# One matmul over both halves of the activations in a three-block transformer kernel

## The chip, the cores and the metric

The kernel runs on one core of one Trainium2 chip. The metric is the time of one execution on the device in microseconds. The change is compared with the kernel before by medians of several executions.

## What is computed

256 tokens of width 1024 in float32 go through a first block and then through a second one of two layers. The first block has a mixer (a gated delta rule and an S5 scan side by side), attention over a memory of 256 rows, and a gated feed-forward layer. Each layer of the second block has a self-attention (stick-breaking and block attention in the first, forgetting attention in the second), attention over a second memory with 4 heads of 64, and a feed-forward layer whose gate and value pass a causal convolution of three taps. All products with weights are in float32, and a root-mean-square norm stands ahead of each. Cut to the second block:

```python
def _rmsnorm(x, gain):
    x32 = x.astype(jnp.float32)
    y = x32 * lax.rsqrt(jnp.mean(x32 * x32, axis=-1, keepdims=True) + EPS)
    return (y * gain.astype(jnp.float32)).astype(x.dtype)
...
def memory_cross_attention(h, mem_h, w_q, w_kv, w_out):
...
    q = (h @ w_q).reshape(B, S, XA_HEADS, XA_HEAD_DIM)
    kv = (mem_h @ w_kv).reshape(B, M, 2, XA_HEADS, XA_HEAD_DIM)
    k, v = kv[:, :, 0], kv[:, :, 1]
    s = jnp.einsum('bshd,bmhd->bhsm', q, k).astype(jnp.float32) * (XA_HEAD_DIM ** -0.5)
    p = jax.nn.softmax(s, axis=-1).astype(h.dtype)
    o = jnp.einsum('bhsm,bmhd->bshd', p, v).reshape(B, S, XA_DIM)
    return o @ w_out
...
def second_block(x, mem, positions, norm_mix_g, norm_xa_g, norm_mem_g, norm_ffn_g,
...
    h = x
    for layer in range(DEPTH_2):
        n = layer // 2
        hn = rmsnorm(h, norm_mix_g[layer])
        if layer % 2 == 0:
            h = h + sb_moba_mixer(hn, positions, ab_w_in[n], ab_w_out[n])
        else:
            h = h + fox_mixer(hn, fox_w_in[n], fox_b_f[n], fox_w_out[n])
        h = h + memory_cross_attention(rmsnorm(h, norm_xa_g[layer]), rmsnorm(mem, norm_mem_g[layer]),
                                       xa_w_q[layer], xa_w_kv[layer], xa_w_out[layer])
        h = h + conv_ffn(rmsnorm(h, norm_ffn_g[layer]), ffn_w_up[layer], ffn_conv_w[layer],
                         ffn_conv_b[layer], ffn_w_down[layer])
    return rmsnorm(h, final_norm_g)
```

## The kernel before

**Tiling.** Activations lie feature by feature: h is 128 partitions x 8 chunks x 256 tokens. A product with a weight of 1024 x 1024 is 8 outputs (m) of 8 blocks (k) of 128 x 128 each. Weights come in slots of 8 blocks (128 x 1024, 512 KB): SyncE loads a slot into w_raw (6 buffers), ScalarE copies it rounded to float32r into w_hi (L1127), and VectorE (L1686) or, for every third slot, GpSimd (L2500) subtracts that from the raw one into w_lo. Both have 3 buffers, and ScalarE waits for the slot three back to be used up before it makes the next w_hi. Activations are split the same way, a_hi by ScalarE (L1153) and a_lo by VectorE (L1698), for attention's outputs b_hi and b_lo.

**Three matmuls per block.** The helper three (L418) multiplies one block of weights: w_hi with x_hi, w_hi with x_lo, w_lo with x_hi, each 256 columns wide and all added up in the same 256 columns of a bank. A bank holds 512 columns of float32. Where the tokens are the stationary side (the value products, tok_slot), the moving side is 512 columns of weights. The first stages (w_in, and the keys and values of the second memory, up to x_v) take raw weights in one matmul.

**Stages in order of time.** w_in with the delta rule and the scan (to 141 us), x_v and x_k (keys and values of the first memory, to about 235), glu, w_out, x_q with attention, x_o, ffn0 (342 to 528), ab_v, ab_q and ab_k with attention, ab_o, m_q0, memory attention, m_o0, ffn1 (693 to 885), fox_v, fox_f, fox_q and fox_k, fox_o, m_q1, memory attention, m_o1, ffn2, the last norm.

**Output projections.** residual, written once for each engine, computes w_out, x_o, ab_o, fox_o (K = 8) and m_o0, m_o1 (K = 2). TensorE's fm makes one output m after the other in two banks in turn. VectorE adds it to h (L2115) and frees the bank, then makes a_lo of the chunk before (L1698) and adds its squares up (L2105; not for m_o0 and m_o1). ScalarE makes a_hi (L1153) and the square (L1143) as soon as h is there. Ahead of each h both engines call ahead, which makes w_hi (ScalarE) or w_lo (VectorE, if the slot is not GpSimd's) up to three slots beyond the one in use. The order within each engine is that of the program text, and every wait is on a semaphore.

**Scaled products.** x_k, x_q, ab_q, ab_k, fox_q, fox_k, m_q0 and m_q1 are read from their bank once and multiplied by the norm's rstd (scaled, L1858). In the feed-forward layers (ffn) the gate and the value of each of 22 steps are two outputs of 8 blocks, read and scaled at L2245; the down product of a step is 8 blocks that add up in banks 4 to 7 over all steps. In ffn0 a SiLU and a product follow; in ffn1 and ffn2 the convolution comes between.

## Time and profile before

| | us |
|---|---|
| median of 3 executions | 1260.03 |
| lowest and highest | 1256.9 and 1260.96 |
| the profiled execution, as timed | 1257.22 |
| its span in the trace | 1255.3 |
| TensorE busy | 1194.8 (95%) |
| VectorE busy | 808.1 (64%) |
| ScalarE busy | 656.8 (52%) |
| GpSimd busy | 265.0 (21%) |

PE is TensorE, DVE VectorE, ACT ScalarE, POOL GpSimd. Matmuls are pipelined: the duration of one overlaps with the next, so its price in a row is the distance from start to start. A time in brackets behind an instruction is how long its engine sat idle before it, and what ended that. L numbers are lines of the kernel before.

### The profile page before, as it was taken

To read this page: it belongs to the slowest core of one execution; us is meant where nothing else is said; L and a number is where in the kernel's file an instruction comes from. 1 tells how busy PE (TensorE), PEld (TensorE's weight loads), DVE (VectorE), ACT (ScalarE), POOL (GpSimd) and SP (SyncE) were. 2 spreads that over 40 slices of the span, in tenths; PEclk is the share of its full clock that TensorE was granted. 3 is DMA by queue.
4 is the path that set the end of the run, shared out by engine and by line. 5 is a ranking of instruction groups with operands and counts; after the bars stand their busy time and mean duration, and the time that the engine had idled before them with its cause. 6 is when DMAs were issued, how large, how long until landed. Compare 5 with 4: busy or idle time off the path is not lost.

```text
span 1255.3 us, 24604 instructions
## 1 busy us (share of the span) xinstructions
PE 1194.8 (95%) x10064; PEld 1119.2 (89%) x10064; DVE 808.1 (64%) x1426; ACT 656.8 (52%) x1128; POOL 265.0 (21%) x172
## 2 busy tenths in 40 slices
PE   7999999899999999999998899999999988999997
PEld 6888778799899999998886899999889877999997
DVE  4886655564655454567866677677665576776776
ACT  3443633653644444465455655555655566555554
POOL 4030000121222322321120222322221211232231
PEclk9999899999999999999999999999999999999999
DMA  8443322353565565643343466565443342656651
GB/s 320 128 134 119 108 96 86 101 169 101 155 199 175 181 189 181 184 135 102 117 135 102 119 200 176 181 192 178 150 141 116 115 151 84 187 182 187 181 176 48
DMA packets 51518, 187.58 MB, mean 149 GB/s; under 512 B 5712, under 2 KB 5840, under 8 KB 51024
## 3 DMA queue, kind: packets, MB, share of 16 engines
q1 hardware_dynamic: 51408, 186.02, 47.8%
q8 instruction: 80, 1.31, 0.4%
q14 instruction: 30, 0.25, 0.1%
HBM read 184.95 MB, written 1.05 MB: 148 GB/s over the span
## 4 chain that ended last, share of the span: by engine, by line
PE 83%; DVE 7%; ACT 4%; issue 3%; POOL 1%; DMA 0%; DVEq 0%; SPq 0%; ACTq 0%
PE banks L418 62%; PE banks L448 7%; ACT w_hi L1127 2%; PE banks L491 2%; DVE w_lo L1686 1%; PE banks L476 1%; PE banks L924 1%; PE banks L938 1%; POOL w_lo L2500 1%; DVE h L2115 1%; PE banks L539 1%; PE banks L904 1%; DVE gates L2105 1%; PE banks L841 1%; DVE a_lo L1698 1%
## 5 line engine op out<-in xcount | busy, mean ns | idle before, releaser
L418 PE MATMUL banks<-a_hi,w_hi 128*128 128x256 f32 x1432 | 412.2, 288 | 10.1 <-ACT arena L1426 4.2
L2500 POOL TENSOR_TENSOR w_lo<-w_raw,w_hi 128x1024 fp32r<-128x1024 f32 x99 | 240.6, 2430 | 836.0 <-ACT w_hi L1127 836.0
L1127 ACT ACTIVATE w_hi<-w_raw 128x1024 fp32r<-128x1024 f32 x313 | 328.4, 1050 | 157.4 <-PE banks L418 157.3
L418 PE MATMUL banks<-a_lo,w_hi 128*128 128x256 f32 x1432 | 405.9, 283 | 0.0
L418 PE MATMUL banks<-a_hi,w_lo 128*128 128x256 f32 x1432 | 405.8, 283 | 0.0
L1686 DVE TENSOR_TENSOR w_lo<-w_raw,w_hi 128x1024 fp32r<-128x1024 f32 x214 | 264.5, 1236 | 66.7 <-ACT w_hi L1127 66.5
L418 PEld LDWEIGHTS banks<-a_hi,w_hi 128*128 128x128 f32 x1432 | 275.4, 192 | 14.9 <-ACT arena L1426 4.6
L418 PEld LDWEIGHTS banks<-a_lo,w_hi 128*128 128x128 f32 x1432 | 275.5, 192 | 0.4
L418 PEld LDWEIGHTS banks<-a_hi,w_lo 128*128 128x128 f32 x1432 | 275.3, 192 | 0.0
L418 PE MATMUL banks<-b_hi,w_hi 128*128 128x256 f32 x880 | 254.9, 290 | 16.2 <-DVE h L2115 3.9
L418 PE MATMUL banks<-b_hi,w_lo 128*128 128x256 f32 x880 | 249.9, 284 | 0.0
L418 PE MATMUL banks<-b_lo,w_hi 128*128 128x256 f32 x880 | 249.9, 284 | 0.0
L418 PEld LDWEIGHTS banks<-b_hi,w_hi 128*128 128x128 f32 x880 | 169.5, 193 | 22.4 <-issue 12.2
L418 PEld LDWEIGHTS banks<-b_lo,w_hi 128*128 128x128 f32 x880 | 169.7, 193 | 0.3
L418 PEld LDWEIGHTS banks<-b_hi,w_lo 128*128 128x128 f32 x880 | 169.6, 193 | 0.0
L1569 ACT ACTIVATE arena<-arena,pars 128x256 f32<-128x256 f32 x88 | 53.0, 602 | 132.9 <-DVE arena L2245 132.9
L2245 DVE TENSOR_TENSOR arena<-banks,rstd 128x256 f32<-128x256 f32 x132 | 55.8, 423 | 103.2 <-PE banks L418 93.4
L448 PE MATMUL banks<-early,w_raw 128*128 128x256 f32 x400 | 92.2, 390 | 7.6 <-DMA w_raw<-in_weights 7.6
L2250 DVE SCALAR_TENSOR_TENSOR arena<-arena,pars 128x255 f32<-128x255 f32 x88 | 59.1, 672 | 60.7 <-ACT arena L1569 60.7
L448 PEld LDWEIGHTS banks<-early,w_raw 128*128 128x128 f32 x400 | 77.0, 195 | 19.4 <-DMA w_raw<-in_weights 7.6
L1153 ACT ACTIVATE a_hi<-h,pars 128x256 fp32r<-128x256 f32 x64 | 32.5, 507 | 63.4 <-DVE h L2115 53.3
L1584 ACT ACTIVATE b_hi<-arena 128x256 fp32r<-128x256 f32 x66 | 27.6, 418 | 36.6 <-DVE arena L2264 36.6
(379 smaller groups left out, 1326.7 us busy)
## 6 DMA issues: line engine op xcount, KB each, us to landing
w_raw<-in_weights SPq DMA_DIRECT2D x342, 512.0 KB, 3.6
h<-in_x SPq DMA_DIRECT2D x1, 1024.0 KB, 5.1
arena<-in_mem SPq DMA_DIRECT2D x1, 1024.0 KB, 12.3
early<-in_mem SPq DMA_DIRECT2D x1, 1024.0 KB, 14.3
out_h<-h SPq DMA_DIRECT2D x4, 256.0 KB, 2.7
...
```

The source lines that it names most:

```text
L418: ins = mm(out, l, r, start=start and n == 0, stop=stop and n == 2, skip_group_check=check)
L448: ins = mm(out, raw(s, b % 8), x[:, k, :], start=n == 0, stop=n == K - 1)
L476: ins = mm(out, x[:, k, cols], raw(s, b * w % 8, w), start=k == 0, stop=k == K - 1)
L491: ins = mm(bank[2][:, 0:T] if out is None else out, ONES_D[:] if by is None else by, squares, start=m == 0, stop=m == KD - 1)
L1127: do(WHI[:, n % SPLIT_SLOTS, :], RAW[:, n % RAW_SLOTS, :], ACT.Copy).then_inc(*inc("w_hi_made", ("w_hi", n)))
L1153: do(x[0][:, m, :], src, ACT.Copy, scale=par(g, m)).then_inc(*inc("input_hi", ("a_hi", tag, m)))
L1569: do(FC[:, 2 * (f % 2) + g, :], FS[:, 2 * (f % 3) + g, :], ACT.Identity, scale=par(f"cw{conv}", 88 + g * NF + f), bias=par(f"cb{conv}", g ...
L1584: do(BH[:, f % 3, :], FA[:, f % 2, :], ACT.Copy).then_inc(*inc("ffn_act_hi", ("act_hi", tag, f)))
L1686: v.tensor_tensor(WLO[:, n % SPLIT_SLOTS, :], RAW[:, n % RAW_SLOTS, :], WHI[:, n % SPLIT_SLOTS, :].bitcast(F32), ALU.subtract).then_inc(*i ...
L2245: v.tensor_tensor(x, acc(t)[:, 0:T], R[:], ALU.mult).then_inc(*inc("ffn_scaled", ("fs", tag, f, g), ("acc", t)))
L2250: step(v.scalar_tensor_tensor(c[:, 1:T], x[:, 0:T - 1], par(f"cw{conv}", 44 + g * NF + f), c[:, 1:T], ALU.mult, ALU.add), label="ffn_conv")
L2500: g.tensor_tensor(WLO[:, n % SPLIT_SLOTS, :], RAW[:, n % RAW_SLOTS, :], WHI[:, n % SPLIT_SLOTS, :].bitcast(F32), ALU.subtract).then_inc(*i ...
```

## The change

The halves of the activations come to lie in one tensor each (a_parts, b_parts, halves outermost). A new helper, joint, takes the place of three in most products with weights as the stationary side: one matmul of w_hi with both halves, 512 columns, into the whole bank, and one of w_lo with x_hi, 256 columns, into its first half. The bank then holds two partial results per output, and its reader adds them: for h two additions with a wait between them (the second frees the bank); in scaled and in ffn0's gate and value a reduction over pairs into the destination, then the multiplication by rstd there. Left as they were: glu, fox_f, the gates and values of ffn1 and ffn2 (ONE_HALF), every down product, and all products with tokens as the stationary side. In this version the matmuls fall from 8766 to 7710 instructions in the program, by 1056. Not shown below are the sites where only x[0] and x[1] became x[:, 0] and x[:, 1] on ScalarE.

```diff
--- before.py
+++ after.py
@@ -235,8 +235,8 @@
                 "p (a b) -> p a b", a=KD) for i in range(3))
         WHI = sb("w_hi", [P, SPLIT_SLOTS, 1024], F32R)
         WLO = sb("w_lo", [P, SPLIT_SLOTS, 1024], F32R)
-        AH, AL = sb("a_hi", [P, KD, T], F32R), sb("a_lo", [P, KD, T], F32R)
-        BH, BL = sb("b_hi", [P, KD, T], F32R), sb("b_lo", [P, KD, T], F32R)
+        A, B = (sb(n, [P, 2, KD, T], F32R) for n in ("a_parts", "b_parts"))
+        (AH, AL), (BH, BL) = ((x[:, 0, :, :], x[:, 1, :, :]) for x in (A, B))
         RAW = sb("w_raw", [P, RAW_SLOTS, 1024])
         H = sb("h", [P, KD, T])
         K1, V1 = sb("k1", [P, KD, T]), sb("v1", [P, TT, D])
@@ -292,8 +292,9 @@
 
             return bank[(6, 6, 6, 6, 6, 2, 3, 4)[p]]
 
-        A = (AH, AL)
-        B = (BH, BL)
+        def halves(key):
+
+            return acc(key).rearrange("p (a b) -> p a b", a=2)
 
 
         QKV = area(0, 12, T)
@@ -418,12 +419,19 @@
                     ins = mm(out, l, r, start=start and n == 0, stop=stop and n == 2, skip_group_check=check)
                 return ins
 
+            def joint(out, w, x, k, start, stop):
+
+
+                mm(out.rearrange("p (a b) -> p a b", a=2), w[0], x[:, :, k, :], start=start, stop=stop,
+                   skip_group_check=True)
+                return mm(out[:, 0:T], w[1], x[:, 0, k, :], start=False, stop=stop, skip_group_check=True)
+
             def blocks(s, b, n=1):
                 c = slice(b * P, (b + n) * P)
                 return WHI[:, s % SPLIT_SLOTS, c], WLO[:, s % SPLIT_SLOTS, c]
 
             def pair(x, k, cols=slice(0, T)):
-                return x[0][:, k, cols], x[1][:, k, cols]
+                return x[:, 0, k, cols], x[:, 1, k, cols]
 
             def raw(s, b, n=1):
                 return RAW[:, s % RAW_SLOTS, b * P:(b + n) * P]
@@ -432,7 +440,7 @@
 
 
                 K = SHAPE[name][0]
-                out = acc_take((name, m))[:, 0:T]
+                out = acc_take((name, m))
                 for n, k in enumerate(range(K)):
                     b = m * K + k
                     s = SLOT[name, b // 8]
@@ -445,9 +453,11 @@
                             sums(k)
                         pe.wait_ge(*at(x_ready(k)))
                     if whole(s):
-                        ins = mm(out, raw(s, b % 8), x[:, k, :], start=n == 0, stop=n == K - 1)
+                        ins = mm(out[:, 0:T], raw(s, b % 8), x[:, k, :], start=n == 0, stop=n == K - 1)
+                    elif name in ONE_HALF:
+                        ins = three(out[:, 0:T], blocks(s, b % 8), pair(x, k), n == 0, n == K - 1)
                     else:
-                        ins = three(out, blocks(s, b % 8), pair(x, k), n == 0, n == K - 1)
+                        ins = joint(out, blocks(s, b % 8), x, k, n == 0, n == K - 1)
                     ev = ([("slot", s)] if (m * K + n) % 8 == 7 else []) + ([(name, m)] if n == K - 1 else [])
                     if ev:
                         ins.then_inc(*inc("product_done", *ev))
@@ -862,12 +872,15 @@
                 for f in range(NF + 1):
                     if f < NF:
                         for g in range(2):
-                            out = acc_take((name, 2 * f + g))[:, 0:T]
+                            out = acc_take((name, 2 * f + g))
                             slot_ready(s)
                             for k in range(KD):
                                 if f == 0 and g == 0:
                                     pe.wait_ge(*at(("a_lo", tag, k)))
-                                ins = three(out, blocks(s, k), pair(A, k), k == 0, k == KD - 1)
+                                if name in ONE_HALF:
+                                    ins = three(out[:, 0:T], blocks(s, k), pair(A, k), k == 0, k == KD - 1)
+                                else:
+                                    ins = joint(out, blocks(s, k), A, k, k == 0, k == KD - 1)
                             ins.then_inc(*inc("product_done", ("slot", s), (name, f, g)))
                             s += 1
                             if f == 0 and g == 0:
@@ -1695,12 +1708,12 @@
 
             def lo_gained(tag, m, x, src, g):
                 dve.wait_ge(*at(("a_hi", tag, m)))
-                v.scalar_tensor_tensor(x[1][:, m, :], src, par(g, m), x[0][:, m, :].bitcast(F32),
+                v.scalar_tensor_tensor(x[:, 1, m, :], src, par(g, m), x[:, 0, m, :].bitcast(F32),
                                        ALU.mult, ALU.subtract).then_inc(*inc("input_lo", ("a_lo", tag, m)))
 
             def lo(tag, m, x, src, key=("a_hi", "a_lo")):
                 dve.wait_ge(*at((key[0], tag, m)))
-                v.tensor_tensor(x[1][:, m, :], src, x[0][:, m, :].bitcast(F32), ALU.subtract).then_inc(
+                v.tensor_tensor(x[:, 1, m, :], src, x[:, 0, m, :].bitcast(F32), ALU.subtract).then_inc(
                     *inc("input_lo", (key[1], tag, m)))
 
             v.memset(ONES_D[:], 1.0 / D).then_inc(*inc("vector_step", "ones"))
@@ -1855,8 +1868,14 @@
             def scaled(name, m, dst, r, scale=1.0):
                 t = (name, m)
                 dve.wait_ge(*at((name, m)))
-                v.scalar_tensor_tensor(dst, acc(t)[:, 0:T], scale, r, ALU.mult, ALU.mult).then_inc(
-                    *inc("scaled_out", (name, "scaled", m), ("acc", t)))
+                if whole(SLOT[name, 0]):
+                    v.scalar_tensor_tensor(dst, acc(t)[:, 0:T], scale, r, ALU.mult, ALU.mult).then_inc(
+                        *inc("scaled_out", (name, "scaled", m), ("acc", t)))
+                    return
+                step(v.tensor_reduce(dst, halves(t).rearrange("p a b -> p b a"), AX.X, ALU.add), ("acc", t),
+                     label="halves_summed")
+                v.scalar_tensor_tensor(dst, dst, scale, r, ALU.mult, ALU.mult).then_inc(
+                    *inc("scaled_out", (name, "scaled", m)))
 
 
             turn = delta_banks(bank)
@@ -2112,7 +2131,8 @@
                     ahead(FIRST[name] + (m * K + K - 1) // 8)
                     t = (name, m)
                     dve.wait_ge(*at((name, m)))
-                    step(v.tensor_tensor(H[:, m, :], H[:, m, :], acc(t)[:, 0:T], ALU.add),
+                    step(v.tensor_tensor(H[:, m, :], H[:, m, :], halves(t)[:, 0, :], ALU.add), label="halves_summed")
+                    step(v.tensor_tensor(H[:, m, :], H[:, m, :], halves(t)[:, 1, :], ALU.add),
                          ("h", tag, m), ("acc", t), label="h_made")
                     if m:
                         lo_gained(tag, m - 1, A, H[:, m - 1, :], g)
@@ -2242,8 +2262,13 @@
                                 dve.wait_ge(*at(("fa", tag, f - 3)))
                             x = FS[:, 2 * (f % 3) + g, :]
                             t = (name, 2 * f + g)
-                            v.tensor_tensor(x, acc(t)[:, 0:T], R[:], ALU.mult).then_inc(
-                                *inc("ffn_scaled", ("fs", tag, f, g), ("acc", t)))
+                            if conv is not None:
+                                v.tensor_tensor(x, acc(t)[:, 0:T], R[:], ALU.mult).then_inc(
+                                    *inc("ffn_scaled", ("fs", tag, f, g), ("acc", t)))
+                            else:
+                                step(v.tensor_reduce(x, halves(t).rearrange("p a b -> p b a"), AX.X, ALU.add), ("acc", t),
+                                     label="halves_summed")
+                                v.tensor_tensor(x, x, R[:], ALU.mult).then_inc(*inc("ffn_scaled", ("fs", tag, f, g)))
                             if conv is not None:
                                 c = FC[:, 2 * (f % 2) + g, :]
                                 dve.wait_ge(*at(("fc", tag, f, g)))
@@ -2579,6 +2604,8 @@
 
 SUMMED = ("xa", "f0", "xa0", "xa1")
 
+ONE_HALF = ("glu", "fox_f", "ffn1", "ffn2")
+
 POOL_SUMMED = ("mem1", "mem2")
 
 sq_before = {}
```

The order of TensorE's instructions in x_o, from its last block into ffn0's first output, before (waits in brackets):

```order
L418 MATMUL banks<-b_hi,w_hi 128x256
L418 MATMUL banks<-b_lo,w_hi 128x256
L418 MATMUL banks<-b_hi,w_lo 128x256
L418 MATMUL banks<-a_hi,w_hi 128x256 [waits w_lo_made,input_lo,w_hi_made,h_made]
L418 MATMUL banks<-a_lo,w_hi 128x256
L418 MATMUL banks<-a_hi,w_lo 128x256
L418 MATMUL banks<-a_hi,w_hi 128x256 [waits input_lo]
```

and after:

```order
L425 MATMUL banks<-b_parts,w_hi 128x512
L427 MATMUL banks<-b_parts,w_lo 128x256
L425 MATMUL banks<-a_parts,w_hi 128x512 [waits w_lo_made,input_lo,w_hi_made,h_made]
L427 MATMUL banks<-a_parts,w_lo 128x256
L425 MATMUL banks<-a_parts,w_hi 128x512 [waits input_lo]
```

Three matmuls became two; the waits stand on the first of each block as before.

VectorE at the end of an output projection and the start of the next stage (x_o, then ffn0), before; squares are added at L2105, w_lo made at L1686:

```order
L1686 TENSOR_TENSOR w_lo<-w_raw,w_hi 128x1024 [waits w_hi_made]
L2115 TENSOR_TENSOR h<-h,banks 128x256 [waits product_done]
L1698 SCALAR_TENSOR_TENSOR a_lo<-h,pars,a_hi 128x256 [waits input_hi,h_made]
L2105 TENSOR_TENSOR gates<-gates,squares 128x256 [waits squares_summed,squares]
L1698 SCALAR_TENSOR_TENSOR a_lo<-h,pars,a_hi 128x256 [waits input_hi]
L2105 TENSOR_TENSOR gates<-gates,squares 128x256 [waits squares_summed,squares]
L2245 TENSOR_TENSOR arena<-banks,rstd 128x256 [waits product_done,rstd]
```

and after:

```order
L1699 TENSOR_TENSOR w_lo<-w_raw,w_hi 128x1024 [waits w_hi_made]
L2134 TENSOR_TENSOR h<-h,banks 128x256 [waits product_done]
L2135 TENSOR_TENSOR h<-h,banks 128x256 [waits halves_summed]
L1711 SCALAR_TENSOR_TENSOR a_parts<-h,pars,a_parts 128x256 [waits input_hi,h_made]
L2124 TENSOR_TENSOR gates<-gates,squares 128x256 [waits squares_summed,squares]
L1711 SCALAR_TENSOR_TENSOR a_parts<-h,pars,a_parts 128x256 [waits input_hi]
L2124 TENSOR_TENSOR gates<-gates,squares 128x256 [waits squares_summed,squares]
L2269 TENSOR_REDUCE arena<-banks 128x256 [waits product_done,rstd]
L2271 TENSOR_TENSOR arena<-arena,rstd 128x256 [waits halves_summed]
```

Between w_lo and a_lo now stand two additions, the second waiting for the first; the event h_made is the second's.

VectorE in m_q0, ahead of the memory attention, before:

```order
L1858 SCALAR_TENSOR_TENSOR arena<-banks,rstd 128x256 [waits product_done,rstd]
L1686 TENSOR_TENSOR w_lo<-w_raw,w_hi 128x1024 [waits w_hi_made]
L1858 SCALAR_TENSOR_TENSOR arena<-banks,rstd 128x256 [waits product_done]
L2138 TENSOR_REDUCE small<-banks 128x2 [waits scores_done] x3
L2146 RECIPROCAL small<-small 128x2 [waits exp_done]
```

and after:

```order
L1875 TENSOR_REDUCE arena<-banks 128x256 [waits product_done,rstd]
L1877 SCALAR_TENSOR_TENSOR arena<-arena,rstd 128x256 [waits halves_summed]
L1699 TENSOR_TENSOR w_lo<-w_raw,w_hi 128x1024 [waits w_hi_made]
L1875 TENSOR_REDUCE arena<-banks 128x256 [waits product_done]
L1877 SCALAR_TENSOR_TENSOR arena<-arena,rstd 128x256 [waits halves_summed]
```

Each scaling is two instructions now; the first reduction waits for the rstd, which only the second instruction needs.

## Rows read from the trace of the kernel before

**Rows 1.** the page: busy time of each engine and TensorE's largest group of matmuls
```profile
PE 1194.8 (95%) x10064; PEld 1119.2 (89%) x10064; DVE 808.1 (64%) x1426; ACT 656.8 (52%) x1128; POOL 265.0 (21%) x172
L418 PE MATMUL banks<-a_hi,w_hi 128*128 128x256 f32 x1432 | 412.2, 288 | 10.1 <-ACT arena L1426 4.2
```

**Rows 2.** stretches; us, busy time (count) per engine, granted clock, DMA share, GB/s
```profile
342.00:517.00 175.00, 174.89 (x1456) 174.57 (x1456) 87.59 (x131) 82.02 (x110) 49.89 (x21) 1.00 0.60 185
549.00:635.00 86.00, 83.86 (x628) 74.53 (x628) 67.54 (x102) 47.36 (x83) 16.82 (x7) 1.00 0.40 117
712.00:882.00 170.00, 170.00 (x1417) 170.00 (x1418) 123.28 (x199) 93.74 (x137) 46.36 (x20) 1.00 0.62 184
920.00:997.00 77.00, 76.39 (x624) 67.71 (x622) 39.02 (x73) 40.82 (x99) 14.82 (x6) 1.00 0.40 124
```

**Rows 3.** order of time, PE, value products within fox: start us, us, engine, line
```profile
984.02 0.39 PE L418 MATMUL banks<-w_hi,a_hi 128*128 128x512 f32 x1
987.88 0.39 PE L418 MATMUL banks<-w_lo,a_hi 128*128 128x512 f32 x1
```

**Rows 4.** order of time, one turn of the loop in x_o, VectorE and ScalarE
```profile
335.72 0.41 DVE L2115 TENSOR_TENSOR h<-h,banks 128x256 f32<-128x256 f32 x1
...
336.17 0.51 ACT L1153 ACTIVATE a_hi<-h,pars 128x256 fp32r<-128x256 f32 x1 [1.62 <-DVE h L2115]
...
336.89 1.04 ACT L1127 ACTIVATE w_hi<-w_raw 128x1024 fp32r<-128x1024 f32 x1
...
337.96 1.23 DVE L1686 TENSOR_TENSOR w_lo<-w_raw,w_hi 128x1024 fp32r<-128x1024 f32 x1 [0.98 <-ACT w_hi L1127]
339.11 0.41 DVE L2115 TENSOR_TENSOR h<-h,banks 128x256 f32<-128x256 f32 x1
```

**Rows 5.** additions into h in w_out, x_o, ab_o, fox_o: busy, mean ns | idle before
```profile
L2115 DVE TENSOR_TENSOR h<-h,banks 128x256 f32<-128x256 f32 x8 | 3.3, 414 | 0.8 <-PE banks L418 0.8
L2115 DVE TENSOR_TENSOR h<-h,banks 128x256 f32<-128x256 f32 x8 | 3.3, 414 | 2.7 <-PE banks L418 2.7
L2115 DVE TENSOR_TENSOR h<-h,banks 128x256 f32<-128x256 f32 x8 | 3.3, 414 | 1.0 <-PE banks L418 1.0
L2115 DVE TENSOR_TENSOR h<-h,banks 128x256 f32<-128x256 f32 x8 | 3.3, 414 | 2.4 <-PE banks L418 2.4
```

**Rows 6.** order of time, VectorE: second h of x_o and of fox_o
```profile
319.21 0.42 DVE L2115 TENSOR_TENSOR h<-h,banks 128x256 f32<-128x256 f32 x1 [2.21 <-PE banks L418]
...
1000.46 0.42 DVE L2115 TENSOR_TENSOR h<-h,banks 128x256 f32<-128x256 f32 x1 [1.66 <-PE banks L418]
```

**Rows 7.** order of time, VectorE in m_o0: two additions in a row
```profile
684.06 0.87 DVE L2115 TENSOR_TENSOR h<-h,banks 128x256 f32<-128x256 f32 x2
```

**Rows 8.** VectorE's reductions over 512 columns of a bank
```profile
L2138 DVE TENSOR_REDUCE small<-banks 128x2 f32<-128x512 f32 x12 | 8.0, 686 | 4.9 <-PE banks L818 4.5 <-PE banks L1033 0.5
```

**Rows 9.** order of time, VectorE in m_q0
```profile
668.72 0.42 DVE L1858 SCALAR_TENSOR_TENSOR arena<-banks,rstd 128x256 f32<-128x256 f32 x1 [2.48 <-ACT rstd L1160]
```

**Rows 10.** order of time, m_o0 and the start of ffn1
```profile
686.83 0.42 DVE L2115 TENSOR_TENSOR h<-h,banks 128x256 f32<-128x256 f32 x1 [0.35 <-PE banks L418]
...
693.44 1.02 DVE L1698 SCALAR_TENSOR_TENSOR a_lo<-h,pars,a_hi 128x256 fp32r<-128x256 f32 x2
...
696.09 0.59 PE L491 MATMUL banks<-squares,ones_d 128*128 128x256 f32 x2
```

**Rows 11.** order of time in x_o: VectorE beside GpSimd
```profile
328.30 2.69 POOL L2500 TENSOR_TENSOR w_lo<-w_raw,w_hi 128x1024 fp32r<-128x1024 f32 x1 [7.01 <-ACT w_hi L1127]
...
328.64 2.64 DVE L2105 TENSOR_TENSOR gates<-gates,squares 128x256 f32<-128x256 f32 x1
```

**Rows 12.** PE after a wait before w_out, and the stretch behind it
```profile
241.46 0.38 PE L418 MATMUL banks<-a_hi,w_hi 128*128 128x256 f32 x1 [4.23 <-ACT arena L1426]
...
241.60:245.10 3.50, 3.50 (x18) 3.50 (x19) 1.09 (x3) 1.59 (x3) 2.31 (x1) 0.53 0.00 0
```

**Rows 13.** order of time, PE: ffn0's first output waits for a_lo
```profile
340.10 0.38 PE L418 MATMUL banks<-a_hi,w_hi 128*128 128x256 f32 x1 [0.81 <-DVE a_lo L1698]
```

4 lines of the change are left out of this document (2 added, 2 removed).

## The prediction

> **What bounds the kernel now.** Read the busy line first: TensorE works in 95% of the span, VectorE in 64% [rows 1]. So nearly everything that shortens TensorE's stream counts, and everything that adds to VectorE is free as long as TensorE does not have to wait. Which of the two holds differs from stage to stage, so the second view is the table of stretches [rows 2]. In ffn0 (342 to 517 us) TensorE is busy 174.89 of 175.00 us with 1456 matmuls, 120.1 ns each, and VectorE only 87.59. ffn1's inner stretch is as dense with VectorE at 123.28 of 170: a VectorE filled to 73% does not hold TensorE there. Attention's ab stretch has VectorE at 67.54 of 86, fox at 39.02 of 77.
>
> The third view, the order of time, shows stages that TensorE does not bound. In the four output projections with K = 8 (w_out, x_o, ab_o, fox_o) the additions into h are 3.39 us apart (335.72 to 339.11) without VectorE waiting for TensorE [rows 4]: h, then ScalarE's a_hi at 336.17, square, w_hi at 336.89, then VectorE's w_lo at 337.96, then the next h. It is a closed loop, since w_hi stands behind the square on ScalarE, and h behind w_lo on VectorE. One block of 24 matmuls needs 24 x 0.120 = 2.88 us, so TensorE is the faster one in such a turn. Where the slot's w_lo is GpSimd's (one in three), the turn is short and VectorE waits for the product: in all 0.8, 2.7, 1.0 and 2.4 us in the four stages [rows 5]. At the end of x_o TensorE already waits 0.81 us for a_lo [rows 13].
>
> **The joint matmul.** A dense matmul of 256 columns takes 120 ns from start to start [rows 2]. For 512 columns, 17 starts from 984.02 to 987.88 are 227 ns apart [rows 3]. Two of 256 columns are 240, so a block of one 512 and one 256 takes 347 instead of 360 ns: 13 ns less. The bounds are 0 (the small one takes 133 ns behind a large one) and 26 (what a small one takes beyond half of a large one and its 13 is hidden too). The change converts 1056 blocks: 352 in ffn0, 64 each in x_k, w_out, x_q, x_o, ab_q, ab_k, ab_o, fox_q, fox_k, fox_o, and 16 each in m_q0, m_o0, m_q1, m_o1. That is 13.7 us of TensorE's time, of which only the blocks in dense stages count.
>
> The rows give a fixed part of some 13 ns per matmul. The Trainium skill, page "TensorE: Matmul & The Clock Gate", section "Back-to-back issue gap", gives N/2.4 + 2.5 ns for matmuls in a row, under which a block would save 2.5 ns, 2.6 us over all 1056; the trace's 120 ns for 256 columns is above its 109, and the trace decides.
>
> **Where the gain stays.** ffn0: 352 x 13 ns = 4.6 us. VectorE gets 44 reductions of 512 columns, at 0.69 us by the nearest row [rows 8], in place of the read of 256, and a multiplication of 0.42 behind it: 44 x 0.73 = 32 us on top of 87.59, 120 of 175, what ffn1 bears without a gap. x_q: 0.8. x_k: 0.8, of which 0.2 stay, since its reductions lie between steps of the delta chain. ab_q and ab_k: 1.7; VectorE grows by 16 x 0.73 = 12 to 79 of 86 [rows 2], so I take 1.1 for stalls, the price of a whole new scaling step once on the path (0 to 5), leaving 0.6. fox_q and fox_k: 1.7 less 0.7 for one reduction ahead of the first scores, 1.0; there VectorE has room (39 of 77). Sum: 4.6 + 0.8 + 0.2 + 0.6 + 1.0 = **7.2 us gained**.
>
> **Output projections.** The second addition and its wait on the first lie in the loop, since a_hi and the square wait for the second. Its price is the pitch of two additions in a row, 0.87 - 0.42 = 0.45 us [rows 7]. Eight are 3.6. VectorE's waits for the product pay part back. In x_o the 2.21 in front of the second h, in fox_o the 1.66 [rows 6], swallow only what the first h lost (0.45); other waits count in full. w_out 3.6 - 0.8 = 2.8; x_o 3.6 - 0.45 - 0.5 = 2.65; ab_o 3.6 - 1.0 = 2.6; fox_o 3.6 - 0.45 - 0.7 = 2.45; together **10.5 us lost**. What TensorE saves in these stages is worth nothing: the last a_lo is late anyway [rows 13]. Queued behind the second addition are a_lo, the sum of squares and the next w_lo; who waits is TensorE's first output of the next stage. Bounds: 4 x 0.45 = 1.8, if only the last h counts, and 4 x 3.6 = 14.4.
>
> **m_o0 and m_o1** (K = 2, six matmuls per output). The same 0.45 per h makes the fourth h end 4 x 0.45 - 0.35 = 1.45 late and the last 3.0. The last a_lo ends at 693.44 + 1.02 = 694.46, and ffn1's first block passes to the sums at 696.09, so 1.4 of it is slack [rows 10]: 1.6 each, **3.2 us lost** (0 to 6).
>
> **m_q0 and m_q1.** The scaling stands between the rstd and the attention scores [rows 9]: 0.69 + 0.05 + 0.42 instead of 0.42, twice, less 0.2 to 0.5 in which w_lo waits for w_hi anyway: 1.0 each, **2.0 us lost** (0 to 3).
>
> **Clock.** TensorE's idle time at the end of an output projection grows from 0.8 to about 3 us. Before w_out it stood for 4.23 us, and then ran at 0.53 of full speed, the level of 1.2 GHz, for 3.5 us [rows 12]; 18 matmuls there cost 3.50 instead of 2.16, so 1.3 us. I take one such fall in the six stage ends: **1.3 us lost** (0 to 8).
>
> **The sum.** -7.2 + 10.5 + 3.2 + 2.0 + 1.3 = +9.8. The profiled execution took 1257.22 us (a span of 1255.3 and 1.9 around it), so 1267.0 beside it. It lies 2.8 below the median of 1260.03 and near the lowest of three (1256.9); the forecast is a little over the sum, **1268 us**.
>
> **Rivals.**
> - *The collisions with GpSimd go, and it gets faster.* In the output projections VectorE operations with two operands in SBUF stand still while GpSimd makes a w_lo: 2.64 us for 0.42 of work [rows 11], and the four stages hold nine such stretches, of 0.9 to 2.3 us and 15 in all. The new additions read a bank and do not stand still (the 32 additions of those stages all take 0.41 [rows 5]). If the later h moves a_lo and the sum out from beside GpSimd in nearly all cases, 14 us come back: 1254. From six avoided stretches on (6 x 1.7 = 10) the loss of 9.8 is gone. Against it: w_hi, which starts GpSimd, hangs on the same h and moves with it. 0.11.
> - *It nearly cancels.* The loop's loss is half, because the second addition fills time in which VectorE stands beside GpSimd: 10.5 becomes 5, no fall of the clock, 4 us less in the two small stages: 1260. 0.13.
> - *A block saves nothing*, the fixed part staying with the load of weights. Then 736 blocks x 13 ns = 9.6 us of the gain fall away: 1278. TensorE's part would show 360 ns per block. Against it: the 227 ns for 512 columns include a load each. By the page's 2.5 ns per block it would be 1275. 0.10.
> - *The reduction is dear.* With two elements per output instead of 256 it may cost 1.4 instead of 0.69: VectorE in ab 67.54 + 16 x 1.4 = 90 > 86, some 10 us there and 3 in m_q: 1281. 0.05.
>
> **How the numbers follow.** The forecast has 0.61 and spans 1263 to 1274. Of it 0.60 is above 1263.8; a measurement of this kernel can tell some 0.3%, 3.8 us, from no change. Slower: 0.60 + 0.15 from the last two rivals = 0.75. Same: the second rival, 0.13, and 0.01: 0.14. Faster: 0.11. The range of 1256 to 1278 leaves out the first rival (0.11) and the dear reduction with the upper part of the third (0.08).
>
> **What would show it.** In the changed profile: ffn0's stretch dense and shorter by about 4.6 us; the additions into h in x_o 3.8 us apart in w_lo turns, and the stage about 2.6 longer; reductions of 0.69; TensorE waiting 2 us and more for a_lo at each stage end; the start of ffn1 later by 1.6 within its stage. Wrong would be: gaps in ffn0 behind a bank, the h pitch still 3.4, or ab's stretch longer than 86.

## Result and the profile after

The changed kernel is slower: a median of 1274.67 us in four runs (1274.03 to 1279.11) against 1259.82 for the kernel before, and a ratio of 1.0134 with a 95% interval of 1.011 to 1.0158. The forecast was 1268 us. The direction and the place of the largest loss were right; the size was not: 14.9 us were lost by the medians, 16.9 by the ratio, where 8 to 10 were forecast. The profiled execution has a span of 1273.4 us against 1255.3, 18.1 more.

The page of the changed kernel, its busy line and the groups that take the place of the three matmuls (compare [rows 1]):

```profile
PE 1193.5 (94%) x9008; PEld 1062.4 (83%) x9008; DVE 899.5 (71%) x1570; ACT 660.2 (52%) x1128; POOL 265.9 (21%) x172
...
L425 PE MATMUL banks<-a_parts,w_hi 128*128 128x512 f32 x704 | 257.7, 407 | 7.6 <-DVE a_parts L1711 6.9
...
L425 PE MATMUL banks<-b_parts,w_hi 128*128 128x512 f32 x352 | 132.0, 414 | 18.7 <-POOL w_lo L2525 9.0
```

TensorE has 1056 instructions less and is busy 1.3 us less. VectorE has gained 91 us. The waits in front of the wide matmuls are now for VectorE and GpSimd: 18.7 us where attention's outputs are multiplied.

VectorE's additions into h mark the ends of the stages, since they come in the same order in both kernels. First the kernel before (start, duration, engine, line; the last addition of w_out, the first behind ffn0, the last of ab_o, the first behind ffn1, the last of fox_o, the first behind ffn2), then the changed one, with x_o's last, which is in [rows 4] for before, as second row:

```profile
272.22 0.41 DVE L2115 TENSOR_TENSOR h<-h,banks 128x256 f32<-128x256 f32 x1
...
527.72 0.42 DVE L2278 TENSOR_TENSOR h<-h,banks 128x256 f32<-128x256 f32 x1 [1.14 <-PE banks L418]
...
664.24 0.41 DVE L2115 TENSOR_TENSOR h<-h,banks 128x256 f32<-128x256 f32 x1
...
887.63 0.42 DVE L2278 TENSOR_TENSOR h<-h,banks 128x256 f32<-128x256 f32 x1 [1.14 <-PE banks L418]
...
1018.97 0.42 DVE L2115 TENSOR_TENSOR h<-h,banks 128x256 f32<-128x256 f32 x1 [0.51 <-PE banks L418]
...
1242.74 0.42 DVE L2278 TENSOR_TENSOR h<-h,banks 128x256 f32<-128x256 f32 x1 [1.14 <-PE banks L418]
```

```profile
276.16 0.42 DVE L2135 TENSOR_TENSOR h<-h,banks 128x256 f32<-128x256 f32 x1
...
345.01 0.42 DVE L2135 TENSOR_TENSOR h<-h,banks 128x256 f32<-128x256 f32 x1
...
532.67 0.42 DVE L2303 TENSOR_TENSOR h<-h,banks 128x256 f32<-128x256 f32 x1 [1.14 <-PE banks L419]
...
673.51 0.42 DVE L2135 TENSOR_TENSOR h<-h,banks 128x256 f32<-128x256 f32 x1
...
899.75 0.42 DVE L2303 TENSOR_TENSOR h<-h,banks 128x256 f32<-128x256 f32 x1 [1.13 <-PE banks L419]
...
1033.92 0.42 DVE L2135 TENSOR_TENSOR h<-h,banks 128x256 f32<-128x256 f32 x1
...
1261.03 0.42 DVE L2303 TENSOR_TENSOR h<-h,banks 128x256 f32<-128x256 f32 x1 [1.13 <-PE banks L419]
```

The differences of these starts give the ledger, with the prediction's terms beside it:

| stretch | before | after | difference | forecast |
|---|---|---|---|---|
| start to w_out's last h | 272.22 | 276.16 | +3.94 | -0.2 + 2.8 = +2.6 |
| x_q, x_o | 66.89 | 68.85 | +1.96 | -0.8 + 2.65 = +1.85 |
| ffn0 | 188.61 | 187.66 | -0.95 | -4.6 |
| ab, ab_o | 136.52 | 140.84 | +4.32 | -0.6 + 2.6 = +2.0 |
| m_q0, m_o0, ffn1 | 223.39 | 226.24 | +2.85 | 1.0 + 1.6 = +2.6 |
| fox, fox_o | 131.34 | 134.17 | +2.83 | -1.0 + 2.45 = +1.45 |
| m_q1, m_o1, ffn2 | 223.77 | 227.11 | +3.34 | 1.0 + 1.6 = +2.6 |
| the end | 12.56 | 12.37 | -0.19 | 0 |
| falls of the clock, no place given | | | | +1.3 |
| sum | | | +18.10 | +9.8 |

Three stretches hold most of the miss: ffn0 (3.65 us), ab (2.3) and fox (1.4). The stretch up to w_out misses 1.3 more; this lies in glu, where TensorE's granted clock stood at 0.50 for seven microseconds (241 to 248) where it had been three and a half before [rows 12], behind the same wait of 4.23 us. It is scatter and not the change: the profiled executions of experiments 2, 3, 5 and 7 show the long fall too, those of 1, 4, 6, 8 and 9 the short one, and glu is the same in all.

**The loop of h is as foretold.** VectorE in x_o after the change, to be compared with [rows 4]:

```profile
340.71 0.42 DVE L2134 TENSOR_TENSOR h<-h,banks 128x256 f32<-128x256 f32 x1
341.16 0.42 DVE L2135 TENSOR_TENSOR h<-h,banks 128x256 f32<-128x256 f32 x1
...
343.42 1.23 DVE L1699 TENSOR_TENSOR w_lo<-w_raw,w_hi 128x1024 fp32r<-128x1024 f32 x1 [0.94 <-ACT w_hi L1140]
344.56 0.41 DVE L2134 TENSOR_TENSOR h<-h,banks 128x256 f32<-128x256 f32 x1
```

One turn takes 3.85 us (340.71 to 344.56) where it took 3.39.

**A joint block saves 7 ns, not 13.** TensorE in ffn0, one joint block and the start of the next:

```profile
403.17 0.40 PE L425 MATMUL banks<-a_parts,w_hi 128*128 128x512 f32 x1
403.40 0.28 PE L427 MATMUL banks<-a_parts,w_lo 128*128 128x256 f32 x1
403.52 0.40 PE L425 MATMUL banks<-a_parts,w_hi 128*128 128x512 f32 x1
```

The wide one holds TensorE for 236 ns and the narrow one for 117 (means over 269 and 252 pairs between 356 and 500 us), together 353; three narrow ones took 360.

**The multiplication of a scaling has changed its operands.** Before, it read a bank and the rstd. Now the reduction reads the bank, and the multiplication reads two operands in SBUF. The view of one line's instructions gives their shortest, median and longest duration in ns, before and after:

```profile
L1858 DVE SCALAR_TENSOR_TENSOR arena<-banks,rstd x44: 406/424/425, 276.7 to 1027.0; 128x256 f32<-128x256 f32 x44
```

```profile
L1877 DVE SCALAR_TENSOR_TENSOR arena<-arena,rstd x44: 424/425/2604, 281.4 to 1042.8; 128x256 f32<-128x256 f32 x44
...
L1875 DVE TENSOR_REDUCE arena<-banks x44: 673/691/693, 280.6 to 1042.1; 128x256 f32<-128x512 f32 x44
```

No multiplication of before took over 425 ns. After the change seven take 1.13 to 2.60 us, 10.4 us more than their work, and each of them stands beside a w_lo of GpSimd. The dearest, with GpSimd's row, and TensorE's wait behind it (L990 rotates the queries and keys; it waits for the bank of the rotation before, which VectorE reads right behind this multiplication, L2343):

```profile
611.94 2.38 POOL L2525 TENSOR_TENSOR w_lo<-w_raw,w_hi 128x1024 fp32r<-128x1024 f32 x1 [9.83 <-ACT w_hi L1140]
...
611.29 0.68 DVE L1875 TENSOR_REDUCE arena<-banks 128x256 f32<-128x512 f32 x1
612.00 2.60 DVE L1877 SCALAR_TENSOR_TENSOR arena<-arena,rstd 128x256 f32<-128x256 f32 x1
...
615.09 0.67 PE L990 MATMUL banks<-arena 128*128 128x256 f32 x2 [1.59 <-DVE arena L2343]
...
616.00:620.00 4.00, 4.00 (x21) 3.31 (x22) 3.90 (x9) 0.81 (x1) 0.00 (x0) 0.58 0.22 87
```

The last row is the stretch behind the gap (us, then busy time and count per engine, granted clock, DMA share, GB/s): the granted clock is 0.58, that is the level of 1.2 GHz for most of it. The Trainium skill has the rule: by "SBUF — State Buffer", section "Who interferes with whom", a VectorE instruction with two SBUF inputs contends with a GpSimd instruction that reads SBUF, and a tensor_reduce never does. The trace agrees on both: of the 96 reductions of two halves some 30 run beside a w_lo, and none takes over 694 ns.

But most of this standing beside GpSimd is not new. In ab the kernel before has seven stretched instructions of VectorE, 9.4 us beyond their work, on a_lo, the rotation, the stick-breaking scores and a norm; after the change there are eight, of 12.1 us, and five of them are the new multiplication. The kernel before, at the same place in ab as the row of 2.60 us above, in the rotation:

```profile
607.97 2.52 DVE L2320 TENSOR_TENSOR arena<-arena 128x256 f32<-128x256 f32 x1
```

In fox they grow from one stretch of 1.8 us to five of 9.0, two of them on the new multiplication and two on one that was there before and has been moved beside a w_lo, the scaling of the attention weights (before, then after):

```profile
L2181 DVE TENSOR_TENSOR arena<-arena,small 128x256 f32<-128x256 f32 (+1 forms) x16 | 8.2, 554 | 0.3
...
L2201 DVE TENSOR_TENSOR arena<-arena,small 128x256 f32<-128x256 f32 (+1 forms) x16 | 12.5, 825 | 0.3
```

### The profile page after: what moved, and what is told of

It reads as the page before. It is cut to its first block, busy times and chain, and to the rows that moved or that the text cites. A ratio compares the mean times of both kernels' runs of the same rounds, so it can differ in the third digit from the quotient of the medians.

```text
span 1273.4 us, 22636 instructions
## 1 busy us (share of the span) xinstructions
PE 1193.5 (94%) x9008; PEld 1062.4 (83%) x9008; DVE 899.5 (71%) x1570; ACT 660.2 (52%) x1128; POOL 265.9 (21%) x172
## 4 chain that ended last, share of the span: by engine, by line
PE 75%; DVE 14%; ACT 6%; issue 3%; DMA 0%; POOL 0%; DVEq 0%; SPq 0%; ACTq 0%
PE banks L419 38%; PE banks L425 12%; PE banks L456 7%; PE banks L427 6%; DVE w_lo L1699 4%; ACT w_hi L1140 2%; PE banks L501 2%; DVE h L2135 1%; DVE gates L2124 1%; PE banks L486 1%; DVE h L2134 1%; DVE arena L1875 1%; DVE a_parts L1711 1%; PE banks L951 1%; PE banks L937 1%
## 5 line engine op out<-in xcount | busy, mean ns | idle before, releaser
L419 PE MATMUL banks<-a_parts,w_hi 128*128 128x256 f32 x1456 | 268.0, 286 | 8.3 <-ACT arena L1439 4.2
L425 PE MATMUL banks<-a_parts,w_hi 128*128 128x512 f32 x704 | 257.7, 407 | 7.6 <-DVE a_parts L1711 6.9
L419 PEld LDWEIGHTS banks<-a_parts,w_hi 128*128 128x128 f32 x1456 | 229.6, 194 | 10.3 <-ACT arena L1439 4.6
L419 PE MATMUL banks<-a_parts,w_lo 128*128 128x256 f32 x728 | 207.0, 284 | 0.0
L419 PE MATMUL banks<-b_parts,w_hi 128*128 128x256 f32 x1056 | 193.2, 283 | 6.8 <-DVE w_lo L1699 3.5
L427 PE MATMUL banks<-a_parts,w_lo 128*128 128x256 f32 x704 | 198.2, 282 | 0.0
L419 PEld LDWEIGHTS banks<-b_parts,w_hi 128*128 128x128 f32 x1056 | 164.3, 191 | 8.7 <-issue 5.8
L425 PEld LDWEIGHTS banks<-a_parts,w_hi 128*128 128x128 f32 x704 | 133.3, 189 | 42.0 <-DVE a_parts L1711 9.5
L425 PE MATMUL banks<-b_parts,w_hi 128*128 128x512 f32 x352 | 132.0, 414 | 18.7 <-POOL w_lo L2525 9.0
L419 PE MATMUL banks<-b_parts,w_lo 128*128 128x256 f32 x528 | 149.4, 283 | 0.0
L419 PEld LDWEIGHTS banks<-a_parts,w_lo 128*128 128x128 f32 x728 | 140.8, 193 | 0.0
L427 PEld LDWEIGHTS banks<-a_parts,w_lo 128*128 128x128 f32 x704 | 134.0, 190 | 0.3
L419 PEld LDWEIGHTS banks<-b_parts,w_lo 128*128 128x128 f32 x528 | 101.0, 191 | 0.0
L425 PEld LDWEIGHTS banks<-b_parts,w_hi 128*128 128x128 f32 x352 | 66.9, 190 | 40.6 <-issue 12.9
L427 PE MATMUL banks<-b_parts,w_lo 128*128 128x256 f32 x352 | 99.3, 282 | 0.0
```

Source lines behind the costliest of these rows:

```text
L419: ins = mm(out, l, r, start=start and n == 0, stop=stop and n == 2, skip_group_check=check)
L425: mm(out.rearrange("p (a b) -> p a b", a=2), w[0], x[:, :, k, :], start=start, stop=stop, skip_group_check=True)
L427: return mm(out[:, 0:T], w[1], x[:, 0, k, :], start=False, stop=stop, skip_group_check=True)
```

## The experiments

Except where before.py is named, they start from a version of the changed kernel in which each product chooses between three matmuls with one addition or scaling, as before, and the joint product with two, by the list ONE_HALF. The stage lengths beside each come from the same additions into h.

**1. ffn0 alone.**

```diff
-ONE_HALF = ("glu", "fox_f", "ffn1", "ffn2")
+ONE_HALF = ("glu", "fox_f", "ffn1", "ffn2", "w_out", "x_o", "ab_o", "fox_o", "m_o0", "m_o1",
+            "x_k", "x_q", "ab_q", "ab_k", "fox_q", "fox_k", "m_q0", "m_q1")
```

> The joint product in the gate and value of ffn0 alone (352 of the 1056 blocks); everything else reads and multiplies as in the kernel before. Theory of the prediction (13 ns per block, VectorE's 44 reductions and multiplications hidden): 4.6 us faster than the kernel before. Theory from the trace of the changed kernel (a joint block has a pitch of 353 ns against 360, so 7 ns): 2.5 us faster. Rival (VectorE's extra 32 us are not hidden, since two of its multiplications stood beside GpSimd): 0 to 2 us slower.

Measured: 1255.85 us against 1256.82, a ratio of 0.9998 (0.9984 to 1.0013). The time can't tell a gain of 0 from one of 2 us, the trace can: ffn0 (337.44 to 524.94) takes 187.50 us where it took 188.61, 1.1 less. TensorE's gaps in it, none of which the kernel before has:

```profile
346.17 0.51 PE L425 MATMUL banks<-a_parts,w_hi 128*128 128x512 f32 x1 [0.32 <-DVE arena L2270]
...
349.86 0.36 PE L419 MATMUL banks<-b_parts,w_hi 128*128 128x256 f32 x1 [0.61 <-ACT w_hi L1140]
...
523.95 0.36 PE L419 MATMUL banks<-b_parts,w_hi 128*128 128x256 f32 x1 [0.45 <-DVE b_parts L2299]
```

352 blocks x 7 ns are 2.5 us; less 0.32 + 0.61 + 0.45 leaves 1.1. In the 170 us between, VectorE's extra 32 us cost nothing. At both ends they do cost: the first two outputs wait for the rstd and are then read one after the other, and at the end nothing lies between the last scaling and the last down product.

**2. The six output projections alone** (the list holds all but these).

> The joint product and the two additions in the six output projections alone (w_out, x_o, ab_o, fox_o, m_o0, m_o1). By the prediction's terms: 10.5 + 3.2 + 1.3 = 15.0 us slower than the kernel before. Theory from the trace of the changed kernel: 2.2, 2.45, 2.3 and 2.4 in the four long ones, 3.2 in each short one, and 1.6 us for a fall of the clock behind x_o: 17 us slower. Rival (most of the loss sits in the scaled products and ffn0): under 8 us.

Measured: 1272.62 us, 15.8 over the kernel before, ratio 1.0122 (1.0098 to 1.0146). By stage, first to last h: w_out +2.63, x_o +2.56, ab_o +2.35, fox_o +2.27, m_o0 +3.20, m_o1 +3.46. ffn1 behind m_o0 is as long as before within 0.1 us (194.54, 194.64). This is nearly the whole loss of the change, and the prediction's three terms for it, 15.0 us, were nearly right in sum.

**3. The scaled products alone.**

> The joint product in the scaled products alone (x_k, x_q, ab_q, ab_k, fox_q, fox_k, m_q0, m_q1). By the prediction's terms: 0.8 + 0.2 + 0.6 + 1.0 gained against 2.0 lost, 0.6 us faster. Theory from the trace of the changed kernel (the new multiplication has two operands in SBUF and stands still beside GpSimd, seven times, 10.4 us in all; one of them opens a gap of 1.6 us on TensorE with a fall of the clock behind it): 2 to 5 us slower, with the loss in the ab stretch.

Measured: 1260.04 us, 3.2 over the kernel before, ratio 1.0019 (1.0003 to 1.0034). x_q is 0.64 us shorter. ab, from the first h behind ffn0 to ab_o's first (525.99 to 641.32), is 1.37 us longer than before, fox 0.51. Eight multiplications stood beside GpSimd, 12.7 us beyond their work. The prediction's terms fall here: they gave a gain of 0.6 us. The clock did not fall in ab, though the same gap of 1.58 us stood there as in the changed kernel.

**4. Two steps without the joint product.**

```diff
 # before.py, residual on VectorE
-step(v.tensor_tensor(H[:, m, :], H[:, m, :], acc(t)[:, 0:T], ALU.add),
+step(v.scalar_tensor_tensor(H[:, m, :], acc(t)[:, 0:T], 0.5, H[:, m, :], ALU.mult, ALU.add))
+step(v.scalar_tensor_tensor(H[:, m, :], acc(t)[:, 0:T], 0.5, H[:, m, :], ALU.mult, ALU.add),
      ("h", tag, m), ("acc", t), label="h_made")
```

> The kernel before with its three matmuls per block, in which h takes each product in two instructions of half the product, the second waiting for the first; the same in the second block's six output projections as in the first. It tells the second addition apart from the joint product. If the second step in the loop is the whole loss of the output projections: as slow as the kernel with the joint product in the output projections alone, within 2 us, some 15 to 18 us over the kernel before. If the joint product carries a part (its larger matmuls hold a bank for longer): clearly less than that kernel, by 4 us and more.

Measured: 1275.31 us, 18.5 over the kernel before, ratio 1.0147 (1.0118 to 1.0177), whose interval overlaps that of the second experiment; the medians are 2.7 us apart, a little more than the 2 expected, the profiled spans 0.1 (1272.1 and 1272.2). VectorE in w_out, the joint product (experiment 2) and then this kernel:

```profile
264.71 0.41 DVE L2135 TENSOR_TENSOR h<-h,banks 128x256 f32<-128x256 f32 x1
265.15 0.42 DVE L2136 TENSOR_TENSOR h<-h,banks 128x256 f32<-128x256 f32 x1
...
267.65 2.60 DVE L2124 TENSOR_TENSOR gates<-gates,squares 128x256 f32<-128x256 f32 x1
```

```profile
264.77 0.42 DVE L2115 SCALAR_TENSOR_TENSOR h<-banks,h 128x256 f32<-128x256 f32 x1
265.22 0.42 DVE L2116 SCALAR_TENSOR_TENSOR h<-banks,h 128x256 f32<-128x256 f32 x1
...
267.73 2.60 DVE L2105 TENSOR_TENSOR gates<-gates,squares 128x256 f32<-128x256 f32 x1
```

The two run alike to 0.1 us over the whole projection, so in the four long projections the second step is the whole loss, and what TensorE saves there is worth nothing. The rows also settle the rival on GpSimd: the sum of squares still stands beside a w_lo for 2.60 us. In a_lo and the sums together such stretches cost 17.3 us before, 19.5 in experiment 2 and 19.1 after the change; in the four long projections, which the rival was about, there are nine again, of 15.9 us in place of 15.0.

**5. ffn0 with the wide ones first.**

```diff
-                                    ins = joint(out, blocks(s, k), A, k, k == 0, k == KD - 1)
+                                    mm(out.rearrange("p (a b) -> p a b", a=2), blocks(s, k)[0], A[:, :, k, :],
+                                       start=k == 0, stop=k == KD - 1, skip_group_check=True)
+                            if name not in ONE_HALF:
+                                for k in range(KD):
+                                    ins = mm(out[:, 0:T], blocks(s, k)[1], A[:, 0, k, :], start=False,
+                                             stop=k == KD - 1, skip_group_check=True)
```

> As the kernel with the joint product in ffn0 alone, but within an output TensorE first runs the eight matmuls of 512 columns (w_hi with both halves), then the eight of 256 (w_lo with x_hi). It asks where the 6 ns per block went that the prediction counted and the trace doesn't show (353 ns per block instead of 347). If the dear thing is the change between the two widths (a wide one behind a narrow one takes 236 ns, not 227): eight blocks take 8 x 347 ns, ffn0 4.6 us shorter than before and 2.1 shorter than with the alternating order. If a wide matmul with the two halves side by side (2 x 256 columns from two places) is itself dearer than one with 512 columns in a row: 236 ns within the wide ones too, and ffn0 as in the alternating order, 2.5 us shorter than before.

Measured: 1256.00 us against 1256.98, ratio 0.9991 (0.9977 to 1.0005). TensorE in ffn0, one output:

```profile
405.04 2.00 PE L883 MATMUL banks<-a_parts,w_hi 128*128 128x512 f32 x8
406.88 1.12 PE L887 MATMUL banks<-a_parts,w_lo 128*128 128x256 f32 x8
407.83 0.40 PE L883 MATMUL banks<-a_parts,w_hi 128*128 128x512 f32 x1
```

Eight wide ones take 1.84 us, 230 ns each, and eight narrow ones 0.95, 119 each: 349 ns per block against 353 in turns and 360 with three. So both readings were half right. A wide one with its halves in two places costs 3 ns more than one with 512 columns in a row [rows 3], where however the moving side is the weights and not the activations, so that the two places are not shown to be the reason. In turns with narrow ones a wide one takes 6 more and the narrow one 2 less.

This run's ffn0 took 187.59 us, no less than in experiment 1, because the clock fell in it: about 0.5 for three of the microseconds from 340 to 343. Experiment 7 has the same ffn0, behind the same wait of 1.58 us, without a fall: 186.42. The fall cost 1.2 us, and the order of the two widths brings 1.1.

**6. ab without GpSimd.** A pair of kernels: before, and experiment 3, each with

```diff
 def lo_on_pool(s):
     if s < FIRST["glu"]:
         return False
+    if FIRST["ab_q"] <= s < FIRST["ab_o"]:
+        return False
```

> The kernel before, in which VectorE and not GpSimd makes all w_lo of the ab stretch (ab_v, ab_q, ab_k): the reference for the next kernel. VectorE gets some eight w_lo of 1.22 us, and loses its stretches beside GpSimd. Every theory: within 4 us of the kernel before; its own time decides nothing, the difference to the next kernel does.

> The joint product in the scaled products alone, with all w_lo of the ab stretch made by VectorE. Theory: ab loses time because the new multiplication has both operands in SBUF and stands still beside GpSimd. Then without GpSimd no multiplication takes over 0.6 us in ab, and ab (from the end of ffn0 to the first h of ab_o) is no longer than in the reference of the same kind, within 0.7 us, where it was 1.5 us longer with GpSimd. Rival (VectorE is simply too full by the reductions): the stretch is longer than in its reference by 2 us and more, since VectorE now has 8 us more to do.

Seven of the nine w_lo that GpSimd made in this stretch go to VectorE; the two at its ends stay. Measured: 1254.89 us (ratio to the kernel before 0.9992, 0.9977 to 1.0007) and 1256.05 us (0.9999, 0.9987 to 1.0011). The multiplications of the ab stretch (545 to 637 us) in the kernel of experiment 3 and in its sister without GpSimd (busy, mean ns | idle before; in the sister all lines stand two lower, so that its L1879 is the multiplication and its L1877 the reduction):

```profile
L1877 DVE SCALAR_TENSOR_TENSOR arena<-arena,rstd 128x256 f32<-128x256 f32 x16 | 14.3, 896 | 0.6
```

```profile
L1879 DVE SCALAR_TENSOR_TENSOR arena<-arena,rstd 128x256 f32<-128x256 f32 x16 | 6.8, 426 | 0.6
...
619.44 0.47 PE L421 MATMUL banks<-w_hi,a_parts 128*128 128x512 f32 x1 [0.95 <-DVE arena L1877]
```

Their mean falls from 896 to 426 ns, so GpSimd's w_lo was what held them. ab is 112.21 us long against 111.31 in the reference of its kind (528.12 to 640.33, 524.02 to 635.33): 0.90 longer, where it was 1.37 with GpSimd. That is just outside the 0.7 of the theory and well under the 2 of its rival. The collisions are a third of ab's loss in this pair. For the rest a queue is the likely cause: the middle of ab was full before. The stretch of 602 to 624 us, where VectorE's busy time is the third, in the kernel before and in the sister without GpSimd:

```profile
602.00:624.00 22.00, 21.72 (x165) 18.70 (x161) 20.16 (x35) 9.72 (x24) 4.78 (x2) 1.00 0.39 119
```

```profile
602.00:624.00 22.00, 20.80 (x120) 16.53 (x119) 20.52 (x41) 11.32 (x32) 0.00 (x0) 1.00 0.29 99
```

20.16 of 22 us, 92%, where the whole stretch showed 79% [rows 2]. There a reduction more has little room, and TensorE waits 0.95 us for the reduction's bank. In the reference without GpSimd VectorE is busy for 19.48 of the same 22 us, and TensorE has no gap there. That the fullness costs the remaining 0.90 us is argued from these rows; no run takes it away.

**7. ffn0 (wide first) and x_q alone.**

> A version that should beat both: the joint product in ffn0 (wide ones first, then narrow ones) and in x_q alone. From the traces so far x_q is 0.6 us shorter with it and ffn0 2.5 to 4.6: 3 to 5 us faster than the kernel before (ratio 0.996 to 0.998). Rival (VectorE's extra work, or the clock behind the start of ffn0, takes it back): no difference.

Measured: 1255.55 us against 1256.98, ratio 0.9989 (0.9974 to 1.0005). The stages are shorter as expected, ffn0 by 2.19 us and x_q by 0.63, but the clock scatters the whole by more.

**8. The same, and ab without GpSimd.**

> The joint product in ffn0 (wide ones first) and x_q alone, and VectorE makes all w_lo of the ab stretch, so that no work of the ab stretch stands beside GpSimd. The traces give: ffn0 1.0 to 1.5 us shorter, x_q 0.6, ab 2.6: 4 to 5 us faster than the kernel before (ratio 0.996 to 0.997). Rival (the times of one program scatter by several us with the clock in the first 250 us, and the gain of each part was never outside the noise of the medians): a ratio of 0.998 to 1.000.

Measured: 1252.24 us (1249.87 to 1257.31) against 1257.25, ratio 0.9964 (0.9951 to 0.9978). This version beats both kernels. ab takes 110.90 us where it took 113.96. The largest part of the gain has nothing to do with the joint product: it is VectorE freed from GpSimd. Experiment 6 has it alone, ab 2.65 us shorter, though its time could not show it: there the stretches beside GpSimd in ab fall from 9.4 us to 1.3.

**9. All but the output projections.**

> The changed kernel with the six output projections (w_out, x_o, ab_o, fox_o, m_o0, m_o1) back at three matmuls and one addition: the joint product in ffn0 and in the scaled products together. If the parts add up: the 0 to 1 us that ffn0 alone gained and the 2.4 to 3.2 us that the scaled products alone lost, so 1.5 to 3 us slower than the kernel before (ratio 1.001 to 1.0025). The prediction's terms: 5.2 us faster (0.996). If the loss of the whole change (17 us) is more than its parts, because the later ends of the output projections disturb ffn0 and ab: no slower than the kernel before.

Measured: 1259.99 us, 2.7 over the kernel before, ratio 1.0026 (1.0015 to 1.0036), where the prediction's terms gave 5.2 gained. fox is 1.84 us longer here and not 0.5: the clock fell in it at 913 us, behind a wait of 2.12. The parts add up: 0.26% here and 1.22% in the projections are 1.48%, the whole change 1.34% (1.1 to 1.58).

## The prediction, point by point

**Where the miss is.** By the medians of the parts, the output projections lost 15.8 us where 15.0 were forecast (experiment 2), the scaled products lost 3.2 where 0.6 were to be gained (experiment 3), and ffn0 gained 1.0 where 4.6 were forecast (experiment 1). So the forecast failed in the gain: some 3.6 us in ffn0 and 3.8 in the scaled products.

**What bounds the kernel: right, with one hole.** Dense stages bear VectorE's work, projections do not. The hole is the average: ab was judged by 67.54 of 86 us, and in its middle VectorE was busy for 20.16 of 22 (experiment 6).

**The joint matmul: the term of 13 ns was too large.** It was put together from the pitch of narrow ones among narrow ones and of wide ones in a row. In the mixture a block saves 7 ns (353 against 360), 7.4 us over 1056 blocks instead of 13.7. The bounds given, 0 and 26, held it. By the Trainium skill's N/2.4 + 2.5 ns ("TensorE: Matmul & The Clock Gate", "Back-to-back issue gap"), which that section gives for isolated matmuls and not, as the prediction has it, for a stream of them, a block would save 2.5 ns, an estimate; the measured value lies between.

**ffn0: 4.6 us forecast, 0.95 measured.** Two steps failed: the 13 ns, and the waits at the ends of the stage, which were put at nothing. 2.1 of the miss are the 7 ns. In experiment 1, 1.4 more went at the two ends. In the changed kernel itself the clock falls at its start, behind a wait of 1.98 us for the last a_lo (experiments 2 and 4 have this wait too, 1.94 and 1.96 us, and no fall):

```profile
346.00 0.51 PE L425 MATMUL banks<-a_parts,w_hi 128*128 128x512 f32 x1 [1.98 <-DVE a_parts L1711]
...
347.00:351.00 4.00, 4.00 (x15) 3.33 (x15) 1.13 (x3) 3.91 (x6) 2.36 (x1) 0.57 0.57 207
```

It shares its cost with the gaps of the start, which a slow TensorE does not see: ffn0 is 187.66 us with the fall and 187.50 without (experiments 1 and 9).

**ab: 0.6 us gain forecast, 1.97 lost.** The step that failed is "one scaling step once on the path" and the rule behind it, that new work reads a bank and so does not stand still. That held for the additions and the reductions, not for the new multiplication. Its stretch of 2.60 us stands before a gap of 1.59 where the stretch of 2.52 in the kernel before left one of 0.28 (at 610.59), and the clock fell behind it. TensorE's idle time in ab grew from 3.06 to 4.18 us, the fall took 1.7 us of full clock, and 128 blocks of 7 ns gave 0.9 back. The fall need not come: experiments 3 and 9 have the same gap without one, and there ab is 1.37 and 0.96 us longer. By experiment 6 a third of the loss without a fall belongs to GpSimd.

**fox: 1.0 us gain forecast, 0.55 lost.** The step that failed is the price of what stands ahead of the first scores, one reduction at 0.7 us. TensorE's wait there grew from 1.21 us to 2.43:

```profile
930.22 0.69 DVE L1875 TENSOR_REDUCE arena<-banks 128x256 f32<-128x512 f32 x1
930.94 0.42 DVE L1877 SCALAR_TENSOR_TENSOR arena<-arena,rstd 128x256 f32<-128x256 f32 x1
931.28 0.15 DVE L1865 COPY rstd_cols<-banks 128x2 f32<-128x2 f32 x1
...
931.65 0.38 PE L951 MATMUL banks<-arena 64*128 64x128 f32 x2 [2.43 <-DVE rstd_cols L1865]
```

Two reductions stand in that queue, one here and one at 923.19, whose multiplication stood beside GpSimd too. In all TensorE's idle time in fox grew by 1.50 us (2.34 to 3.84), and 0.9 came back by the 7 ns.

**x_k and x_q: right.** x_k shows no clear change, x_q 0.6 us instead of 0.8.

**Output projections: right.** 2.8, 2.65, 2.6 and 2.45 were forecast; from the first h to the last it is 2.64, 2.55, 2.36 and 2.28. Experiment 4 shows the mechanism.

**m_o0: 1.6 us forecast, 3.2 measured.** The step that failed is the slack of 1.4. It was read between the last a_lo and the sums behind ffn1's first block. But TensorE reaches that block only through m_o0's two banks, which each h frees, so it is late itself. Its waits for h in m_o0 before were 0.75 and 1.19 us; the second of them, and then both after the change:

```profile
690.69 0.38 PE L418 MATMUL banks<-b_hi,w_hi 128*128 128x256 f32 x1 [1.19 <-DVE h L2115]
```

```profile
693.89 0.50 PE L425 MATMUL banks<-b_parts,w_hi 128*128 128x512 f32 x1 [1.22 <-DVE h L2135]
...
701.26 0.50 PE L425 MATMUL banks<-b_parts,w_hi 128*128 128x512 f32 x1 [2.29 <-DVE h L2135]
```

Nothing of the 3.2 comes back in ffn1, which is 194.65 us long against 194.64. Part of it is the clock, which fell at 702 us, inside m_o0. In experiment 4, without the joint product and without a fall there, m_o0 is 2.85 longer and ffn1 0.61 shorter, 2.2 together. So 2.2 belong to the second step, in place of 1.6, and about 1.0 to the fall. This fall does go with the change: the wait of 2.29 us stands six times in the traces of the changed kernel and of experiments 2 and 4 (m_o0 and m_o1 of each), and a fall follows it in five. The prediction had one fall for all stage ends and none inside these two stages.

**m_q0: right, and hidden.** From ab_o's last h to m_o0's first it is 19.46 us, 0.36 less than before. But the profiled execution of before had a fall of the clock there. Three kernels with the old m_q0 and without a fall there take 18.6 (experiments 1, 2 and 5), so 0.85 us were lost, where 1.0 was forecast. m_q1, with no fall before or after, takes 20.91 us against 20.54: 0.4 in place of 1.0.

**Clock: 1.3 us forecast, too little.** Summed over single microseconds, TensorE lacked 12.2 us of full speed before and 16.3 after. Much of that is scatter: in the first 260 us alone the lack is 3.4 to 10.2 us over the profiled executions of these kernels, in stages where many have the same instructions. The falls behind longer waits, at 347, 616 and 702 us, are not all the change's: only the third comes back with its wait in other runs. That the falls at 347 and 616 belong to the change is not shown.

**The rivals.** "It nearly cancels" is refuted: the turn of the loop grew by the full 0.46 us. "A block saves nothing" gave 1278 us: a block saves about half of what was counted. "The reduction is dear" is refuted: 691 ns against the 0.69 us forecast. "The collisions with GpSimd go" is refuted by experiment 4's rows: they stayed in the projections and grew in ab and fox. The prediction had asked only which collisions the change would remove, not which it would make.
